# Two products instead of three when attention weighs its values: a head's high and low values side by side in one stationary operand, the two halves added on VectorE, and the squares two steps behind the sums

## What is computed

```python
h   = _rmsnorm(x, norm1_g[l])
proj = h @ w_in[l]
...
outs.append(jnp.einsum('bhqk,bhkd->bhqd', p, v[:, :, :q1]))              # fox, per block of 128 queries
...
outs.append(jnp.einsum('bhqk,bhkd->bhqd', jnp.exp(log_a), v[:, :, :q1])) # stick-breaking
...
mix = jnp.concatenate([_rmsnorm(_from_heads(fox), g_fox[l]),
                       _rmsnorm(_from_heads(sb), g_sb[l])], axis=-1)
x = x + mix @ w_out[l]
x = x + _moe(_rmsnorm(x, norm2_g[l]), ...)
```

## Time and profile before

| | |
|---|---|
| time of the profiled execution | 1456.45 us |
| its span (first to last instruction) | 1454.6 us |
| median of the timed executions | 1456.1 us (1455.57 to 1456.11) |
| TensorE busy | 1427.3 us, 98% of the span |
| VectorE busy | 1315.1 us, 90% |
| ScalarE busy | 1104.3 us, 76% |
| GpSimd busy | 440.1 us, 30% |

### The profile page before, as it was taken

The page is one execution under the profiler, slowest core; times in us unless marked ns, Lnnn a source line. Parts: engine busy times, 40 slices in busy tenths (PEclk is TensorE's granted clock), DMA queues, the critical chain, the costliest instruction groups (busy, mean ns, idle before and its releaser), DMA issues.

```text
span 1454.6 us, 22413 instructions
## 1 busy us (share of the span) xinstructions
PE 1427.3 (98%) x7078; PEld 1161.0 (80%) x7078; DVE 1315.1 (90%) x1528; ACT 1104.3 (76%) x1349; POOL 440.1 (30%) x178
## 2 busy tenths in 40 slices
PE   9999999999999999999999999999999999999996
PEld 7777787787888888888888888888888888888884
DVE  5778766689999999999999999999999999999997
ACT  5668554467888888888888888888888888888885
POOL 3000000051433333444333334444333333334321
PEclk9999999999999999999999999999999999999998
DMA  8021022469999999999999999999999999999963
GB/s 258 12 80 59 30 88 72 107 234 392 409 392 399 399 390 388 383 384 380 380 379 389 374 380 386 374 382 378 368 385 380 378 380 378 369 385 381 377 241 127
DMA packets 98317, 451.88 MB, mean 311 GB/s; under 512 B 11427, under 2 KB 23715, under 8 KB 65506
## 3 DMA queue, kind: packets, MB, share of 16 engines
q1 hardware_dynamic: 90962, 434.68, 77.7%
q0 software_dynamic: 7312, 16.63, 5.0%
HBM read 440.99 MB, written 18.48 MB: 316 GB/s over the span
## 4 chain that ended last, share of the span: by engine, by line
PE 86%; DVE 9%; ACT 3%; issue 2%; DMA 0%; SPq 0%; DVEq 0%; ACTq 0%
PE zpair L2243 48%; PE bank L2243 23%; PE bank L1942 2%; PE bank L1830 2%; PE bank L1832 2%; PE bank L1831 2%; DVE stage_lo L1237 2%; PE bank L2201 1%; PE bank L2193 1%; DVE lbuf L1317 1%; PE zpair L2212 1%; DVE pt_lo L1326 1%; DVE lbuf L1313 0%; DVE cols L1334 0%; PE zpair L1830 0%
## 5 line engine op out<-in xcount | busy, mean ns | idle before, releaser
L1237 DVE TENSOR_TENSOR stage_lo<-ring,stage_hi 128x1024 fp32r<-128x1024 f32 x796 | 945.5, 1221 | 37.9 <-ACT stage_hi L801 10.3
L801 ACT CAST stage_hi<-ring 128x1024 fp32r<-128x1024 f32 x796 | 828.2, 1054 | 168.4 <-PE zpair L2243 133.8
L676 POOL DMA_INDIRECT x_scratch<-qk,sidx x31 | 250.5, 8079 | 264.0 <-ACT qk L1120 264.0
L2243 PE MATMUL zpair<-stage_hi,act_hi 128*128 128x512 f32 x1024 | 322.6, 396 | 0.3 <-DVE act_lo L1642 0.3
L2243 PE MATMUL zpair<-stage_hi,act_lo 128*128 128x512 f32 x1024 | 316.8, 391 | 0.0
L2243 PE MATMUL zpair<-stage_lo,act_hi 128*128 128x512 f32 x1024 | 315.9, 390 | 0.5 <-DVE stage_lo L1237 0.5
L2243 PEld LDWEIGHTS zpair<-stage_lo,act_hi 128*128 128x128 f32 x1024 | 192.0, 188 | 42.8 <-DVE stage_lo L1237 1.4
L2243 PEld LDWEIGHTS zpair<-stage_hi,act_lo 128*128 128x128 f32 x1024 | 192.2, 188 | 41.1
L2243 PEld LDWEIGHTS zpair<-stage_hi,act_hi 128*128 128x128 f32 x1024 | 187.2, 188 | 43.0 <-issue 7.3
L2243 PE MATMUL bank<-stage_hi,act_hi 128*128 128x512 f32 x510 | 159.9, 395 | 0.0
L2243 PE MATMUL bank<-stage_lo,act_hi 128*128 128x512 f32 x510 | 157.1, 389 | 0.0
(11 more groups left out here) (310 smaller groups left out, 1432.9 us busy)
## 6 DMA issues: line engine op xcount, KB each, us to landing
ring<-in_w SPq DMA_DIRECT2D x384, 1024.0 KB, 9.2
ring<-in_w_in SPq DMA_DIRECT2D x12, 1024.0 KB, 5.3
ring<-in_w_out SPq DMA_DIRECT2D x4, 1024.0 KB, 4.8
xs_all<-in_x SPq DMA_DIRECT2D x4, 512.0 KB, 6.8
ring<-in_x SPq DMA_DIRECT2D x4, 512.0 KB, 3.6
tn_scratch<-qk SPq DMA_DIRECT2D x4, 512.0 KB, 2.8
x_scratch<-ring SPq DMA_DIRECT2D x4, 512.0 KB, 4.2
ring<-x_scratch SPq DMA_DIRECT2D x4, 512.0 KB, 5.8
```

What stands on the lines that cost most here:

```text
L676: nc.gpsimd.indirect_dma_start(out=x2_d[:, :], out_offset=bass.IndirectOffsetOnAxis(ap=sidx[:, 0:1], axis=0), in_=yout, in_offset=None, bo ...
L801: nc.scalar.copy(dst, src).then_inc(split_hi, 1)
L1237: nc.vector.tensor_tensor(dst, src, hi_ap.bitcast(F32), ALU.subtract).then_inc(split_lo, 1)
L2243: mm = pe.matmul(bank[b0 + h][:], w[:, k, :], m[:, j % STAGES, h * BANK:(h + 1) * BANK], start=start and w is T_hi and m is stage_hi, stop ...
```

## The change

The values of a pair are stored as `v_parts`, per block of keys four pieces of 64 columns: high of head 0, low of head 0, low of head 1, high of head 1. A stationary operand of 128 columns is now one head's high and low values side by side, so one pass over `pt_hi` and one over `pt_lo` give the products of both parts: high ones in the head's own 64 rows of its bank, low ones in the other 64. They are added afterwards: ScalarE copies the other half of each bank across to `mixed` (the memory of `f_max`), VectorE adds the own half to it. The scaled high part, the low part and the square are then made from `mixed`, 128 rows at a time. These are spread over three steps: s mod 4 = 1 moves and sums, 2 rounds and makes the low part, 3 squares and adds the squares. The last fox pair keeps three products and the old order (`mix_last`).

The diff's core:

```diff
-        v_hi = over("v_hi", [P, 2, TT, P], F32R, qk_at + 16384)
-        v_lo = over("v_lo", [P, 2, TT, P], F32R, qk_at + 20480)
+        v_parts = over("v_parts", [P, 2, TT, 4, HD], F32R, qk_at + 16384)
+        def v_part(p, low):
+            if p == 2 * PAIRS - 1:
+                return v_parts[:, p % 2, :, 2 * low:2 * low + 2, :]
+            return v_parts[:, p % 2, :, 1:3, :] if low else v_parts[:, p % 2, :, 0:4:3, :]
...
# ScalarE
-            def mix_evac(kind, c):
+            def mix_move(kind, c):
+                at = pair_at(kind, c)
+                act.wait_ge(*((pvs_done, TT * (c + 1)) if kind else (pvf_done, c + 1)))
+                if at:
+                    act.wait_ge(mix_added, at)
+                    act.wait_ge(mix_sq, at // 2)
+                    wait(act, sq_added, 3 * (1 - kind) + max(c - 1, 0))
+                else:
+                    act.wait_ge(c_split, 2)
+                for m in range(2):
+                    half, other = slice(64 * m, 64 * m + 64), slice(64 - 64 * m, 128 - 64 * m)
+                    nc.scalar.copy(mixed[half, :], obank[m][other, :]).then_inc(mix_copied, 1)
+            def mix_round(kind, c):
                 hi_t = stick_hi if kind else fox_hi
+                act.wait_ge(mix_added, pair_at(kind, c) + 2)
+                nc.scalar.activation(hi_t[:, c, :], mixed, ACT.Copy,
+                                     scale=gmix[:, 4 * kind + c:4 * kind + c + 1]).then_inc(mix_copied, 2)
+            def mix_square(kind, c):
+                act.wait_ge(mix_added, pair_at(kind, c) + 4)
...
+                nc.scalar.activation(mixed if c else sq_sum[kind], mixed, ACT.Square).then_inc(mix_sq, 2)
...
             for s in range(STEPS + 1):
                 evacuate((s, True))
-                if s > STICK and s % TT == 1 and s > STICK + TT:
-                    mix_evac(0, (s - STICK - TT) // TT)
+                if s > STICK + TT and s % TT:
+                    (mix_move, mix_round, mix_square)[s % TT - 1](0, (s - STICK - TT) // TT)
+                elif s == STICK + 3:
+                    mix_square(1, PAIRS - 1)
...
-                if TT < s < STICK + TT and s % TT == 1:
-                    mix_evac(1, s // TT - 1)
-            mix_evac(0, PAIRS - 1)
+                if TT < s < STICK + 3 and s % TT:
+                    (mix_move, mix_round, mix_square)[s % TT - 1](1, s // TT - 1)
+            mix_last()
# VectorE, at the same steps
+            def mix_sum(kind, c):
+                for m in range(2):
+                    half = slice(64 * m, 64 * m + 64)
+                    dve.wait_ge(mix_copied, pair_at(kind, c) + m + 1)
+                    nc.vector.tensor_tensor(mixed[half, :], obank[m][half, :], mixed[half, :], ALU.add).then_inc(mix_added, 1)
+            def mix_rest(kind, c):
+                dve.wait_ge(mix_copied, pair_at(kind, c) + 4)
+                nc.vector.scalar_tensor_tensor(out=lo_t[:, c, :], in0=mixed, scalar=gmix[:, 4 * kind + c:4 * kind + c + 1],
+                                               in1=hi_t[:, c, :].bitcast(F32), op0=ALU.mult, op1=ALU.subtract).then_inc(mix_added, 2)
+            def add_squares(kind, c):
...
+                dve.wait_ge(mix_sq, pair_at(kind, c) // 2 + 2)
+                nc.vector.tensor_tensor(sq_sum[kind][:], sq_sum[kind][:], mixed[:], ALU.add).then_inc(sq_added, 1)
# TensorE
-                        for w, x in ((v_hi, pt_hi), (v_hi, pt_lo), (v_lo, pt_hi)):
-                            mm = pe.matmul(obank[m][:, kb * P:S], w[:, ph % 2, kb, :],
+                        if ph == 2 * PAIRS - 1:
+                            ways = ((0, pt_hi), (0, pt_lo), (2, pt_hi))
+                        else:
+                            ways = ((2 * m, pt_hi), (2 * m, pt_lo))
+                        for n, (g, x) in enumerate(ways):
+                            mm = pe.matmul(obank[m][:, kb * P:S], v_parts[:, ph % 2, kb, g:g + 2, :].rearrange("p g d -> p (g d)"),
```

More of the change, by code:

```diff
@@ L124, in out_filled, with pair_at @@
     return max(0, streamed(q) - FILLS)
+def pair_at(kind, c):
+    return 4 * (PAIRS * (1 - kind) + c)
 def out_done_at(j):
@@ L233, in build @@
         sq_sum = [f_sum, f_neg]
-        sq_new = f_max
+        mixed = f_max
         qk2 = qk[:].rearrange("p (a b) t -> p a (b t)", b=2)
@@ L860, in v_evac @@
                     act.wait_ge(*((pvs_done, TT * (p - 1)) if p < 6 else (pvf_done, p - 5)))
-                nc.scalar.copy(v_hi[:, p % 2], b.rearrange("p (t d) -> p t d", t=TT)).then_inc(proj_hi, 1)
+                nc.scalar.copy(v_part(p, 0), b.rearrange("p (t m d) -> p t m d", t=TT, m=2)).then_inc(proj_hi, 1)
             def forget_gate():
@@ L932, in mix_evac, with mix_last @@
+            def mix_last():
+                at = pair_at(0, PAIRS - 1)
+                act.wait_ge(pvf_done, PAIRS)
                 for m in range(2):
                     half = slice(64 * m, 64 * m + 64)
[L934 to L939, removed]
@@ L940, in mix_evac @@
-                last = not kind and c == PAIRS - 1
+                    nc.scalar.activation(fox_hi[half, PAIRS - 1, :], obank[m][half, :], ACT.Copy,
+                                         scale=gmix[half, PAIRS - 1:PAIRS]).then_inc(mix_copied, 1)
+                act.wait_ge(sq_added, 3 + PAIRS - 2)
                 for m in range(2):
                     half = slice(64 * m, 64 * m + 64)
[L943 to L946, removed]
+                    act.wait_ge(mix_added, at + m + 1)
+                    nc.scalar.activation(mixed[half, :], obank[m][half, :], ACT.Square).then_inc(mix_sq, 1)
@@ L1355, in pt_lo_part @@
                                         pt_hi[:, :, i:4 * i + 1:3, :].bitcast(F32), ALU.subtract).then_inc(pt_lo_r, 1)
[L1357 to L1361, removed]
+            def mix_sum(kind, c):
                 for m in range(2):
                     half = slice(64 * m, 64 * m + 64)
[L1364 to L1372, removed]
-                    ins = nc.vector.tensor_tensor(sq_sum[kind][:], sq_sum[kind][:], sq_new[:], ALU.add).then_inc(sq_added, 1)
-                    if c == PAIRS - 1:
-                        dve.wait_ge(sq_added, 3 * (2 - kind))
-                        dve.sem_inc(sq_summed, 1)
@@ new lines, in add_squares @@
+            def add_squares(kind, c):
+                if c == 0:
+                    return
+                if c > 1:
+                    dve.wait_ge(sq_added, 3 * (1 - kind) + c - 1)
+                dve.wait_ge(mix_sq, pair_at(kind, c) // 2 + 2)
+                nc.vector.tensor_tensor(sq_sum[kind][:], sq_sum[kind][:], mixed[:], ALU.add).then_inc(sq_added, 1)
+                if c == PAIRS - 1:
+                    dve.wait_ge(sq_added, 3 * (2 - kind))
+                    dve.sem_inc(sq_summed, 1)
@@ L1462, in _ @@
                     pt_lo_part(s - 1)
-                if s > STICK + TT and s % TT == 2:
-                    mix_lo_part(0, (s - STICK - TT) // TT)
+                if s > STICK + TT and s % TT:
+                    (mix_sum, mix_rest, add_squares)[s % TT - 1](0, (s - STICK - TT) // TT)
+                elif s == STICK + 3:
+                    add_squares(1, PAIRS - 1)
                 if s == FIRST_V:
@@ L1476, in _ @@
                     forget_gate((0, None, 1, 2)[s - F_STEP])
-                if TT < s < STICK + TT and s % TT == 1:
-                    mix_lo_part(1, s // TT - 1)
+                if TT < s < STICK + 3 and s % TT:
+                    (mix_sum, mix_rest, add_squares)[s % TT - 1](1, s // TT - 1)
             dve.wait_ge(wrt_in, 32)
             nc.vector.tensor_tensor(wrg, wrt, g2col.unsqueeze(2).to_broadcast([P, KT, E]), ALU.mult).then_inc(wrg_ready, 1)
-            mix_lo_part(0, PAIRS - 1)
+            mix_last()
             for h in range(2):
@@ L1928, in turn_stick @@
                 if i == 1:
-                    wait(pe, mix_lo, 2 * c)
+                    if c:
+                        pe.wait_ge(mix_added, pair_at(1, c - 1) + 2)
                 elif i:
@@ L1999, in sums @@
                 pe.wait_ge(sq_summed, 2 - kind)
-                pe.wait_ge(mix_lo, 2 * PAIRS * (2 - kind))
+                pe.wait_ge(mix_added, pair_at(1, PAIRS) if kind else pair_at(0, PAIRS - 1) + 2)
                 for t in range(TT):
@@ L2084, in _ @@
             pe.wait_ge(split_lo, MOE0)
-            pe.wait_ge(mix_lo, 4 * PAIRS)
+            pe.wait_ge(mix_added, pair_at(0, PAIRS - 1) + 2)
             for j in range(4):
```

23 lines of the change are left out of this document (16 added, 7 removed).

## The result

The changed kernel takes 1448.57 us (median of 5 executions, 1448.10 to 1449.13) where the kernel before takes 1455.99 beside it (5 executions): a ratio of 0.995, interval 0.9936 to 0.9965, or 7.4 us less. The forecast was 6.7 less. The profiled execution took 1448.31 us, its span 1446.6.

The account below looks back on a forecast made before the run. TensorE was taken to bound attention, closely followed by VectorE in the stick-breaking part. Gains of 0.4 + 1.0 + 2.2 + 1.26 + 0.9 + 0.95 = 6.7 us gave a median of 1449.4 us, range 1445.6 to 1453.4.

Parts of the forecast that it names:

- The product: TensorE's `weigh`: dropping the third product saves 1.26 us a pair, 8.8 us over seven pairs.
- rival 1: TensorE alone decides, VectorE keeps up everywhere, longer fox waits go too: 10.2 us less, 1445.9; chance 0.22.
- rival 2: VectorE's low part costs 1.53 us instead of 0.69, in five places: 2.5 us less, 1453.6; chance 0.13.
- rivals 2 and 3: Low part costs 1.53 us (1453.6, chance 0.13); ScalarE's cross-partition copy costs two passes, slower (1459.1, chance 0.05).
- Stick-breaking pairs: Periods between the four stick-breaking `weigh`s: gains of 0.4 us for the first, 1.0 for the second and third together.
- moves up by 2.5 us: VectorE's line 1313 at 114.74, waiting for ScalarE's line 876, starts 2.5 us earlier with the squares gone.
- bounded by ScalarE, 1.2 up: VectorE at 121.03 needs ScalarE's lines 876 to 880, which move only by TensorE's 1.26; VectorE gains 1.2 us.
- Where TensorE waits: TensorE's waits for `pt_lo` before the second to fourth `weigh` grow by some 0.7 us.
- no idle time: Stick-breaking stretch from line 1313 to the next `weigh`: VectorE never idles, so the added 0.69 us low part counts.
- First period: First to second `weigh`: copies wait for `c_all`, line 876 starts 1.1 us earlier, VectorE adds 0.69; gain 0.4 us.
- Fourth `weigh` to the first fox one: The 1.19 us score wait goes, plus 1.26 for the product, less 0.3 for the sum of squares: 2.2 us.
- Fox pairs: Three periods between fox `weigh`s: gains of 1.26, 0.9 (new square in the chain) and 0.95 us.

Follow-up runs that it names:

- e2: Kernel before, with only its third product left out in seven pairs, order unchanged; 1446.96 us, ratio 0.9936.
- e1: Changed kernel with a third product put back in the seven pairs (the `pt_lo` product made twice); 1457.70 us, ratio 1.0014.
- e7: Changed kernel with ScalarE copying each bank's own half, so no copy crosses partitions; 1448.59 us, ratio 0.9948.
- e3: Changed kernel with low part, square and sum of squares of the first three stick-breaking pairs moved behind the next `weigh`; 1450.37 us, ratio 0.9961.
- e5: Changed kernel with low part, square and sum of squares of three stick-breaking pairs behind the next `weigh`, two buffers for the sum; 1447.71 us, ratio 0.9942.
- e4: Changed kernel without the first pair's wait for `c_all` ahead of its two crossed copies; 1446.31 us, ratio 0.9932.
- e6: Changed kernel with fox squares behind ScalarE's Exp and `stage_hi`, their sum behind VectorE's `stage_lo`; 1448.10 us, ratio 0.9946.
- e9: Changed kernel without the first `c_all` wait, fox squares later, two stick-breaking pairs' low part and squares behind next `weigh` with two sum buffers; 1444.80 us, ratio 0.9921.

## Why the prediction was right, and where it was not

**The product.** It was put at 1.26 us a pair, 8.8 in all. The row shows 1.29, and e2 9.0 at the end. The estimate from the Trainium skill ("TensorE: Matmul & The Clock Gate", Back-to-back issue gap), 7.6, is too low here: the trace's own pace decided. That other work returns part of the gain, the ground of the forecast against rival 1, is shown twice: 1.7 us by e1, 1.6 by the distance from e2. (Rival 1's price counts 1.4 us for two fox waits whose rows add up to 2.4, so by its own words it would be 11.2 us less; and the range, meant to reach to rivals 1 and 2, ends 0.2 below rival 2's 1453.6. Neither bears on the result.)

**The prices.** Sum 0.69 forecast and 0.70 measured; low part 0.69 and 0.74; sum of squares 0.69 and 0.68; copy 0.69 and 0.58. The copy lies even below its lower bound of 0.60. So rivals 2 and 3 were out, and e7 shows that the crossing is free, which no row of before could.

**Stick-breaking pairs.** The sum was right (0.56, 0.47, 0.32 against 0.4, 0.5, 0.5), and so was its ground: the new order costs 0.7 to 1.0 us in each of these periods (e1, e2), where the prediction had VectorE's added 0.69. But two steps of its working failed. First, "moves up by 2.5 us" for the line at 114.74: measured from `weigh` it moved from 11.33 to 9.94, by 1.39, because ScalarE's softplus, freed from the squares, found its scores not there yet and waits 1.23 for TensorE. Second, the next of these lines was to be bounded by ScalarE, 1.2 up. ScalarE's L891 is done at 118.48; VectorE starts L1348 at 118.87, straight from its own queue with the low part in it. It gained 0.91 (17.62 to 16.71 behind `weigh`). That the second period still came out at the forecast 0.5 is luck: from this line to the `pt_lo` that releases `weigh` VectorE takes 0.45 us more (10.19 for 9.74), not the 0.69 that was counted for the sum of squares. VectorE's queue, unbroken from 112.10 on, is the bound, as the prediction had it for the stretch as a whole. e3 shows it by experiment for the first two periods and e5 for the third: they shrink by 0.56, 0.74 and 0.98 (e5) when low part and sum of squares leave it. ScalarE's square moves with them there, but in the unbroken stretch VectorE waits for nothing that stands behind it.

**Where TensorE waits.** Forecast: 0.7 us longer for `pt_lo` before the second to fourth `weigh`. Before the second it is 0.76 against 0.68; before the third it was 0.23 and is gone, and before the fourth it is 0.1 in both kernels. The time appears earlier, where the projection needs the bank that VectorE's v part still reads: 0.87 at 128.69, where before had none, and 1.37 at 155.21, where it had 0.38 (at 157.25). The same queue is late, but another reader meets it first. For the third period the prediction took over "no idle time" from the second without a row of its own: VectorE idles 2.52 us just ahead of the last `pt_lo`, at 158.54, as it did before the change (at 160.59), because it waits there for ScalarE's `pt_hi`, which follows TensorE's transposes. So one of the prediction's signs for rival 1, a VectorE that idles before a `weigh`, showed without rival 1's gain. The queue before that, unbroken from 139.65 to 155.07, holds TensorE up at 155.21.

**First period.** The softplus starts 9.78 us behind `weigh` in place of 11.01, 1.2 earlier where 1.1 was forecast. The largest single wait in the period is that of the copies for `c_all`. The prediction counted it inside its 0.4 and did not single it out; e4 puts it at 2.4 us. It is no cost of the new order alone, for the kernel before waits there too, 1.87 us ahead of its squares; against e2, which keeps the old order, the first period is 0.71 longer. Without the wait the changed kernel is 0.65 us below e2. What the old order would gain without it was not tried.

**Fourth `weigh` to the first fox one.** Forecast 2.2, measured 2.40. The wait at the score went as the prediction said: the maximum starts 6.98 us behind the fourth `weigh` in place of 9.98. The 0.3 us for the sum of squares was not needed: it runs at 178.00, behind the `pt_lo` that TensorE wants, and no wait for it shows. The way there is the one period in which the new order itself gains: 1.13 by e1, 1.12 by e2. e3 and e5 put work back on the way to that maximum and lose 2.0 and 1.2 us there.

**Fox pairs.** 1.27, 1.03, 1.08 against 1.26, 0.9, 0.95. In the first the new order costs nothing (0.02 and -0.06 by e1 and e2), as forecast. The square in the second period was put at some 0.36; e6 shows 0.65, about the whole square. That the forecast was still near is luck: the new order as a whole costs 0.24 to 0.29 there. The forecast stood near the result because the wait at the score stayed at 1.20 (1.23 before) instead of growing. What shortened that chain by as much was not tried by itself. In the third, the wait grew from 0.65 to 1.15 by the rows, yet 0.13 more was gained than forecast; why the new order costs only 0.16 to 0.24 there stays open.

## What to carry to other kernels

Work taken off the bound engine returned whole here where what replaces it does not stand in a queue that this engine waits for (first fox period), and by a quarter to under a half where it does (stick-breaking): count the replacement at the place in the queue, not by its sum. Work that passes between two engines several times (copy, add, round, subtract, square) should be spread over steps, so that each engine finds its input ready; done in one go for three pairs it ate nearly the whole gain here, over half of it behind the first pair, where the steps also stood behind the wait for `c_all`. When work is moved into idle time, look at whose buffer it then holds: in e3 waits for a buffer (2.0 us at the third and fourth pair) outweighed the idle time won. And look at what a wait protects: nothing needed the one for `c_all` (3.2 us), and e4 without it is 2.3 us shorter.

## What the runs showed of the hardware

In the profiled execution of e9 TensorE's clock fell in the router, in work that has the full clock throughout in the changed kernel's trace. Windows of 6 us (columns as above):

```profile
286.00:292.00 6.00, 6.00 (x43) 5.49 (x43) 5.20 (x7) 3.65 (x7) 3.95 (x2) 1.00 0.60 240
292.00:298.00 6.00, 6.00 (x47) 5.30 (x46) 5.29 (x21) 4.73 (x11) 0.77 (x2) 1.00 0.66 261
298.00:304.00 6.00, 5.85 (x47) 5.12 (x45) 4.67 (x21) 4.64 (x9) 0.80 (x2) 0.69 0.64 215
304.00:310.00 6.00, 6.00 (x37) 4.44 (x36) 4.00 (x14) 2.46 (x3) 1.95 (x3) 0.50 0.26 84
310.00:316.00 6.00, 6.00 (x58) 5.46 (x56) 5.92 (x8) 0.94 (x3) 3.05 (x7) 0.95 0.46 150
```

The granted clock goes from 1.00 (2.4 GHz) to 0.50 (1.2 GHz) and back, although TensorE was busy 5.85 of 6 us or more in each of these windows. The time behind the last `weigh` is 1177.89 us in that execution and 1175.30 in the changed kernel's (1175.1 to 1175.5 in all other profiled executions), so the fall cost about 2.6 us; the other four executions of e9 took 1444.61 to 1444.97. What set it off stays open. It is a reason to read the median and the periods, not one execution's span.
